# Cached keys turned by VectorE in 32x32 blocks in place of TensorE, in a decoder trunk on one core

## The chip, the cores and the metric

The kernel runs on one core of a Trainium2 chip. The core has five engines with instruction streams of their own: TensorE (PE; its weight loads are shown as PEld), VectorE (DVE), ScalarE (ACT), GpSimd (POOL) and SyncE (SP), which here only issues DMAs. They wait for each other by semaphores. The metric is the device time of one execution, in microseconds; lower is better.

## The reference

One inference step of two decoder layers with shared weights: a prompt of 1024 positions, and 8 samples with 8 new positions each. Layer 0 is a recurrent mixer and an FFN, layer 1 dilated windowed attention with 16 heads of 64 and an FFN. The change touches the attention of the samples. Each has 2048 cached keys and values:

```python
def dilated_gather(q, kall, vall, d, span):
    kidx = NP + jnp.arange(S)[:, None] - d * j[None, :]
    ...
    s = jnp.einsum('bshd,bsjhd->bhsj', q, kg) * (q.shape[-1] ** -0.5)
    s = s - alibi_slopes()[:, None, None] * (d * j)[None, None, :]
    ...
    o = jnp.einsum('bhsj,bsjhd->bshd', p, vg) / den.transpose(0, 2, 1)[..., None]
```

for three patterns (128 positions with stride 1, 512 with 4, 2048 with 16), combined by their softmax denominators. The kernel computes the union of the three as one softmax with a bias that holds slopes and multiplicities (`c_bs`), over 1280 cached positions and 8 new ones.

## The kernel before

All work is in one program with hand-written order. After the QKV projection (`s8_*`) comes the attention stage (`s9_*`). Its unit is a **slot** n: one pair of heads and one block of 128 queries of the prompt, qb = n % 8, so with (qb+1) x 128 key columns. There are 64 slots; slots -5 to -1 hold only sample work and the first queries and keys. Slots -5 to -2 are run by TensorE between the last 16 units of the projection (`run_in`, L2051). A slot has four phases on TensorE (`step`, L2529): the score matmuls of the block, then "turns" (128x128 transposes by matmul with the identity, up to four into one PSUM bank, `turn`, L2424), the product of the probabilities of slot n-2 with the values (`pv`), and sample work.

The **sample work** is laid over the slots: eight slots, s = 0 to 7, serve one sample b (`sample_slot`); s = (qb + 5) % 8. A sample has ten tiles of cached keys and ten of values, each 128 positions x 1024 numbers (all heads), 512 KB. In s = 0 to 4 four units of keys are turned (two tiles, eight transposes each, `turns`, L2277), ScalarE copies them to `smp_kt` (L2559), and TensorE scores them against a block matrix of the queries (`tile_scores`, L2472) in phase 3. VectorE adds the bias and takes minima (`piece`, L2651). In s = 5 the exponentials follow, in s = 6 the sample's probabilities are turned, in s = 7 they are multiplied with the ten value tiles (L2524), and `weigh` (L2657) normalizes in s = 0 of the next sample.

**The prompt's work by engine in slot n.** VectorE: `att_scores` reduction of both heads (L2677, with the bias and minimum), reciprocal, then copies of turned probabilities of slot n-1 (`take`, L2636), `piece`, and the output product of slot n-2 (L2708). ScalarE: copies of turned keys and queries in between the exponentials (L2583). GpSimd spreads reciprocals and issues loads of q, k, v and bias. The exponentials of n wait for the reduction of n, the turns of probabilities in slot n+1 for the exponentials of n.

**Turning banks.** Four PSUM banks serve the turns, but two of them hold scores while qb is 4 to 7, and are then given to turns from phase 3 on only. The plan gives each unit the bank that was longest unused:

```python
rest = () if n < 0 else (2,) if n >= NSLOT else (2, 3) if n % QT < 4 or f >= 3 else ()
x = min((0, 1) + rest, key=lambda b: last_use[b])
```

TensorE waits, before it turns into a bank, for the copy of what was there (`t_out`). Units are taken two per phase, in the order of the list that `turns` makes: the key units first, then those of the next pair's queries and keys, then the probabilities.

**The tiles' loads** are issued by SyncE in order of use (`cache_load`, L2363), into 10 buffers (12 near the end); a load waits for the last use of its buffer, and SyncE issues nothing behind it meanwhile. Key and value tiles 8 and 9 of a sample are put together from four loads each.

## Time and profile before

| | |
|---|---|
| time, median of 3 runs | 2775.1 us (2773.65 to 2776.35) |
| profiled execution | 2772.5 us, of which the trace's span is 2770.7 |
| TensorE busy | 2719.8 us |
| VectorE, ScalarE, GpSimd busy | 1737.5, 945.5, 97.6 us |
| DMA | 254.6 MB in 126388 packets |
| attention stage, slots from -1 on | from about 1500 us to about 1915 us |
| granted clock of TensorE, mean | 0.998 |

Busy times are shares of one profiled execution. A chain view follows the work back from the last instruction; a timeline lists merged runs of instructions with start and length; a windows view gives the busy time of each engine in a stretch, the granted clock, the mean busy share of the 16 DMA engines and GB/s.

### The profile page before, as it was taken

How to read it: one execution, taken by the hardware profiler on the slowest of the kernel's cores; microseconds unless marked ns; L12 is line 12 of the kernel's file. 1: busy time of each engine (PE TensorE's matmuls, PEld its weight loads, DVE VectorE, ACT ScalarE, POOL GpSimd, SP SyncE). 2: the span in 40 equal slices, each digit the busy share in tenths (PEclk: the TensorE clock that was granted, in tenths of full speed). 3: DMA queues.
4: the chain of work that ended last, by engine and by line, in shares of the span. 5: the costliest groups of instructions: out<-in, count | busy, mean ns of one | idle time of the engine just before them, and what ended most of it. 6: DMA issues, size and time to landing. Idle time of an engine off the chain costs nothing.

```text
span 2770.7 us, 56587 instructions
## 1 busy us (share of the span) xinstructions
PE 2719.8 (98%) x24537; PEld 2614.3 (94%) x24537; DVE 1737.5 (63%) x2858; ACT 945.5 (34%) x1690; POOL 97.6 (4%) x220
## 2 busy tenths in 40 slices
PE   7999999999999999999999999999999999999998
PEld 7998999999999999999998777777999999999998
DVE  5754536777777777755521666657377776766676
ACT  5543523322222222432223555554232222222222
POOL 1010000000000000000011111100000000000000
PEclk9999999999999999999999999999999999999999
DMA  5120120011111111133355776863101111111112
GB/s 201 34 82 13 64 99 31 31 50 58 46 47 46 47 47 47 62 127 95 95 176 193 258 268 218 281 238 127 61 16 47 47 47 46 47 47 47 57 52 80
DMA packets 126388, 254.64 MB, mean 92 GB/s; under 512 B 7617, under 2 KB 88725, under 8 KB 125632
## 3 DMA queue, kind: packets, MB, share of 16 engines
q1 hardware_dynamic: 112944, 189.26, 20.7%
q0 software_dynamic: 11888, 57.25, 5.9%
q10 hardware_dynamic: 1312, 4.52, 0.5%
q8 instruction: 196, 3.21, 0.5%
q14 instruction: 48, 0.39, 0.0%
HBM read 222.98 MB, written 28.02 MB: 91 GB/s over the span
## 4 chain that ended last, share of the span: by engine, by line
PE 92%; DVE 4%; ACT 2%; DMA 1%; issue 1%; POOL 0%; ACTq 0%; DVEq 0%; POOLq 0%
PE psum L1574 30%; PE psum L1629 18%; PE psum L483 14%; PE psum L224 11%; PE psum L1549 3%; PE psum L2459 2%; PE psum L2503 2%; PE psum L2419 2%; PE psum L2444 2%; PE psum L2472 1%; PE psum L2524 1%; DVE att_scores L2677 1%; DMA x_natural<-in_x_prompt 1%; PE psum L592 1%; PE psum L2448 1%
## 5 line engine op out<-in xcount | busy, mean ns | idle before, releaser
L1810 DVE TENSOR_TENSOR x_res<-x_res,psum 128x544 f32<-128x544 f32 x352 | 250.4, 719 | 155.4 <-PE psum L1629 155.4
L483 PE MATMUL psum<-w_hi,h_hi 128*128 128x256 f32 (+1 forms) x1152 | 327.1, 284 | 1.0 <-ACT qkv_tok L2074 1.0
L483 PE MATMUL psum<-w_hi,h_lo 128*128 128x256 f32 (+1 forms) x1152 | 323.6, 281 | 0.0
L483 PE MATMUL psum<-w_lo,h_hi 128*128 128x256 f32 (+1 forms) x1152 | 322.9, 280 | 0.0
L1629 PE MATMUL psum<-ffn_hi,ffn_unit_hi 128*128 128x272 f32 x1408 | 292.6, 289 | 1.8 <-DVE x_res L1810 1.4
L1629 PE MATMUL psum<-ffn_lo,ffn_unit_hi 128*128 128x272 f32 x1408 | 291.5, 288 | 0.0
L1629 PE MATMUL psum<-ffn_hi,ffn_unit_lo 128*128 128x272 f32 x1408 | 290.8, 288 | 0.0
L1574 PE MATMUL psum<-h_hi,ffn_unit_lo 128*128 128x272 f32 x1280 | 265.2, 288 | 0.0
L1574 PE MATMUL psum<-h_lo,ffn_unit_hi 128*128 128x272 f32 x1280 | 264.8, 288 | 0.0
L1574 PE MATMUL psum<-h_hi,ffn_unit_hi 128*128 128x272 f32 x1280 | 264.5, 288 | 0.0
L1629 PEld LDWEIGHTS psum<-ffn_hi,ffn_unit_hi 128*128 128x128 f32 x1408 | 220.7, 188 | 3.2 <-DVE x_res L1810 3.2
L1629 PEld LDWEIGHTS psum<-ffn_lo,ffn_unit_hi 128*128 128x128 f32 x1408 | 220.8, 188 | 0.0
L1629 PEld LDWEIGHTS psum<-ffn_hi,ffn_unit_lo 128*128 128x128 f32 x1408 | 220.7, 188 | 0.0
L483 PEld LDWEIGHTS psum<-w_hi,h_hi 128*128 128x128 f32 (+1 forms) x1152 | 215.1, 187 | 4.1 <-issue 1.8
L483 PEld LDWEIGHTS psum<-w_lo,h_hi 128*128 128x128 f32 (+1 forms) x1152 | 215.2, 187 | 0.0
L483 PEld LDWEIGHTS psum<-w_hi,h_lo 128*128 128x128 f32 (+1 forms) x1152 | 215.0, 187 | 0.0
L1574 PEld LDWEIGHTS psum<-h_hi,ffn_unit_hi 128*128 128x128 f32 x1280 | 201.0, 188 | 0.0
L1574 PEld LDWEIGHTS psum<-h_hi,ffn_unit_lo 128*128 128x128 f32 x1280 | 200.7, 188 | 0.0
L1574 PEld LDWEIGHTS psum<-h_lo,ffn_unit_hi 128*128 128x128 f32 x1280 | 200.6, 189 | 0.0
L1574 PE MATMUL psum<-ffn_t_hi,ffn_unit_lo 128*128 128x272 f32 x960 | 198.6, 288 | 0.0
L1574 PE MATMUL psum<-ffn_t_hi,ffn_unit_hi 128*128 128x272 f32 x960 | 198.6, 288 | 0.0
L1574 PE MATMUL psum<-ffn_t_lo,ffn_unit_hi 128*128 128x272 f32 x960 | 198.5, 288 | 0.0
(385 smaller groups left out, 5261.9 us busy)
## 6 DMA issues: line engine op xcount, KB each, us to landing
cache_tile<-in_cache_k SPq DMA_DIRECT2D x64, 512.0 KB, 8.2
cache_tile<-in_cache_v SPq DMA_DIRECT2D x64, 512.0 KB, 13.2
w_raw<-in_w_ffn_gate SPq DMA_DIRECT2D x22, 1024.0 KB, 5.1
w_raw<-in_w_ffn_up SPq DMA_DIRECT2D x22, 1024.0 KB, 5.1
w_raw<-in_w_ffn_down SPq DMA_DIRECT2D x22, 1024.0 KB, 4.8
w_raw<-in_w_in_att SPq DMA_DIRECT2D x12, 1024.0 KB, 7.1
w_raw<-in_w_in_rec SPq DMA_DIRECT2D x10, 1024.0 KB, 4.8
park_x<-x_res POOLq DMA_DIRECT2D x2, 4368.0 KB, 13.3
```

The source lines that it names most:

```text
L224: mm = pe.matmul(PS[:, bank + c, 0:n], st[slot][:, wc:wc + P], mv[:, k, c * CW:c * CW + n], start=(i < NCH), stop=(i >= 3 * NCH * nk - NCH))
L483: mm = pe.matmul(PS[0:n, bank, 0:BW], st[:, k, w:w + n], mv[slot][:, k * BW:(k + 1) * BW], start=(k == 0 and x == 0) if used is None else ...
L592: pe.matmul(PS[:, bank, 0:n], wt[:, j, :], XC[j % 2][:, c * CW:c * CW + n], start=True, stop=True).then_inc(g_in, 1)
L1549: mm = pe.matmul(PS[:, 2 * s + c, 0:CC], st[slot][:, k * BW + f * P:k * BW + (f + 1) * P], mv[:, k, t * TH + c * CC:t * TH + (c + 1) * CC] ...
L1574: mm = pe.matmul(PS[:, 2 * s + c, 0:CC], st[i % NU][:, k * P:(k + 1) * P], mv[:, k0 + k, t * TH + c * CC:t * TH + (c + 1) * CC], start=(fr ...
L1629: mm = pe.matmul(PS[:, 2 * s + c, 0:CC], st[(w0 + m // 2) % NU][:, x:x + P], mv[:, f, t * TH + c * CC:t * TH + (c + 1) * CC], start=(n < 2 ...
L1810: dve.tensor_tensor(x, x, pset(dset(g, i)), ALU.add).then_inc(s_res, 1)
L2419: mm = pe.matmul(PS[:, 2 * e + c // 512, 0:min(512, W - c)], q[p % 2][e * DH:(e + 1) * DH, qb * P:(qb + 1) * P], k[p % 2][e * DH:(e + 1) * ...
L2444: mm = pe.transpose(to[:, h * P:(h + 1) * P], TILE[BUF[j]][:, hp * P:(hp + 1) * P], ident[:, :])
L2448: mm = pe.transpose(to[:, t * P:(t + 1) * P], (QN, KN)[c // 2][:, 4 * (c % 2) + t, :], ident[:, :])
L2459: mm = pe.transpose(to[:, (k - c) * P:(k - c + 1) * P], SX[x % 2][:, e, y * P:(y + 1) * P], ident[:, :])
L2503: mm = pe.matmul(PS[c:c + NQ, 6, 0:P], VN[p % 2][:, x, c:c + NQ], PT[:, m % 2, c // DH * (qb + 1) + x, :], start=(x == 0), stop=(x == qb), ...
```

## The change

The key units vanish from TensorE's turns and from ScalarE's copies. VectorE turns each key tile with one instruction, 32x32 block by block, straight from the loaded tile into `smp_kt`. To make that fit, a key tile is loaded in another form: partition 32x+i holds head group x (four heads) of positions 32a+i, for four a. That takes four loads of 128 KB with pieces of 1 KB for every key tile. Rows and columns of the sample's queries, bias (`c_bs`), value product and output are reordered to match. VectorE turns two tiles at the end of its slots s = 7, 0, 1, 2, 3, for the next slot's scores; the first pair of sample 0 comes before slot -5. ScalarE takes the copies of the turned probabilities whose column offset is 4 or 12 blocks.

```diff
-        if b is not None:
-            units += [("k", i // 2, i % 2) for i in range(K_AT[s], K_AT[s + 1])]
...
-        return unit[0] not in ("p", "s") or unit[0] == "s" and unit[2] == 1
+        return unit[0] not in ("p", "s") or unit[0] == "s" and unit[2] == 1 or unit[0] == "p" and unit[2] % 8 == 4
...
+    def turned_at(b, x):
+
+        return 8 * b + x - 1 - LEAD
...
+            if u < 10:
+                for x in range(4):
+                    rows = sk[:, b, t, :, 256 * x:256 * x + 256] if t < 8 else sk[:, b, t:16:2, 3, 256 * x:256 * x + 256]
+                    sp.dma_start(TILE[BUF[j]][32 * x:32 * x + 32, :].rearrange("p (a d) -> p a d", a=4),
+                                 rows).then_inc(b_tile[BUF[j]], 16)
...
         def tile_scores(b, t):
-            bank, count = k_last(b, t)
-            pe.wait_ge(t_out[bank], count)
+            pe.wait_ge(b_kt, 10 * b + t + 1)
...
-            mm = sample_scores(lambda hp: SKT[:, t % 2, hp, :], (t % 2) * P, P)
+            mm = sample_scores(lambda x: SKT[:, t % 2, :, x, :], (t % 2) * P, P)
...
+        elif what == "p":
+            k = min(4, 2 * (x % QT + 1) - c)
+            act.activation(PT[:, x % 2, c:c + k, :].rearrange("p a w -> p (a w)"), bank[:, 0:k * P],
                            ACT.Copy).then_inc(t_out[TB_[g]], 1)
...
     def s9_dve(dve):
+        def keys(b, x):
+            if b or x:
+                dve.wait_ge(b_sc, 5 * b + x)
+            for t in (2 * x, 2 * x + 1):
+                j = 20 * b + t
+                dve.wait_ge(b_tile[BUF[j]], load_due(j))
+                dve.transpose(SKT[:, t % 2, :, :, :].rearrange("p a b w -> p (a b w)"), TILE[BUF[j]][:, :]).then_inc(b_kt, 1)
+
+        keys_at = {turned_at(b, x): (b, x) for b in range(DB) for x in range(5)}
+        dve.wait_ge(wl_done, B_QKV + N_QKV)
+        keys(0, 0)
...
                 dve.tensor_tensor(OX[:, m // QT, (m % QT) * P:(m % QT + 1) * P], PS[:, 6, 0:P], RS[:, n % 2, :],
                                   ALU.mult).then_inc(a_ox, 1)
+            if n in keys_at:
+                keys(*keys_at[n])
```

Beside this, the query and key rows of the samples are loaded by eight small DMAs of GpSimd in place of two, the four copies of `q_blocks` take 32 partitions each, and the two final copies of the samples' outputs become four each.

## Rows read from the trace of the kernel before

**Rows 1.** The page: busy time and count by engine; the chain by engine.
```profile
PE 2719.8 (98%) x24537; PEld 2614.3 (94%) x24537; DVE 1737.5 (63%) x2858; ACT 945.5 (34%) x1690; POOL 97.6 (4%) x220
...
PE 92%; DVE 4%; ACT 2%; DMA 1%; issue 1%; POOL 0%; ACTq 0%; DVEq 0%; POOLq 0%
```

**Rows 2.** Windows: one period, slot by slot; stretch, length, busy by engine, clock, DMA.
```profile
1661.04:1665.35 4.31, 4.31 (x82) 3.70 (x81) 3.13 (x11) 1.16 (x5) 0.30 (x1) 1.00 0.25 70
1665.35:1670.48 5.13, 5.13 (x93) 4.44 (x93) 4.00 (x13) 3.36 (x7) 1.30 (x6) 1.00 0.01 3
1670.48:1678.30 7.82, 7.82 (x117) 4.63 (x117) 4.24 (x14) 3.26 (x11) 0.29 (x1) 1.00 0.49 167
1678.30:1683.40 5.10, 5.10 (x97) 4.47 (x93) 3.32 (x9) 3.51 (x9) 0.29 (x1) 1.00 1.02 410
...
sum 51.49, PE 50.43 PEld 40.45 DVE 32.28 ACT 28.43 POOL 6.57; mean PE 6.30 PEld 5.06 DVE 4.03 ACT 3.55 POOL 0.82
```

**Rows 3.** The chain at the end of the projection: start, length, what.
```profile
1446.71 0.87 PE psum L2444 x8
...
1450.93 1.05 ACT smp_kt L2559 x2
...
1502.15 9.81 DMA out_v_sample<-qkv_tok
```

**Rows 4.** Timeline of slot s3: start, length, engine, line, what.
```profile
1698.04 1.09 PE L2444 MATMUL psum<-ident,cache_tile 128*128 128x128 f32 x8
1698.15 1.09 DVE L2677 CUSTOM_DVE_ANT_0 att_scores<-psum,att_bias 128x896 f32<-128x896 f32 x1 [0.81 <-PE psum L2419]
...
1701.01 1.29 DVE L2636 COPY att_pt<-psum 128x512 f32<-128x512 f32 x2 [0.67 <-PE psum L2459]
...
1701.24 0.27 PE L2496 MATMUL psum<-ident,att_rden_cols 128*128 128x128 f32 x1
...
1703.55 0.66 PE L2459 MATMUL psum<-ident,att_scores 128*128 128x128 f32 x4
```

**Rows 5.** Groups by line and form, 1380 to 2000 us: busy, mean ns, idle before.
```profile
L2444 PE MATMUL psum<-ident,cache_tile 128*128 128x128 f32 x640 | 87.6, 281 | 8.9 <-ACT smp_kt L2559 7.3 <-DMA cache_tile<-in_cache_k 1.5
L2559 ACT ACTIVATE smp_kt<-psum 128x512 f32<-128x512 f32 x160 | 86.9, 598 | 117.3 <-PE psum L2444 117.3
...
L2472 PE MATMUL psum<-smp_kt,smp_q_blocks 128*32 128x128 f32 x1280 | 43.1, 273 | 0.4 <-ACT smp_kt L2559 0.2
...
L2677 DVE CUSTOM_DVE_ANT_0 att_scores<-psum,att_bias 128x1024 f32<-128x1024 f32 x16 | 19.0, 1222 | 6.2 <-PE psum L2419 6.2
```

**Rows 6.** Groups by line and form, VectorE, whole span, from SBUF to SBUF.
```profile
L210 DVE TENSOR_TENSOR w_lo<-w_raw,w_hi 128x2048 fp32r<-128x2048 f32 x34 | 77.8, 2288 | 38.2 <-ACT w_hi L206 38.0
...
L1084 DVE TENSOR_TENSOR_SCAN lru_sa<-lru_a,lru_i 128x1092 f32<-128x1092 f32 x4 | 9.7, 2429 | 0.1
...
L1833 DVE TENSOR_SCALAR ffn_t<-x_res,vec_cols 128x544 f32<-128x544 f32 x8 | 3.6, 496 | 0.0
```

**Rows 7.** Timeline of slot s7, loads and VectorE's last; landing of all cached tiles.
```profile
1673.26 4.30 SPq L2385 DMA_DIRECT2D cache_tile<-in_cache_k  x8
...
1675.72 0.28 DVE L2708 TENSOR_TENSOR att_out<-psum,att_rden_rows 128x128 f32<-128x128 f32 x1
...
1677.60 1.86 SPq L2388 DMA_DIRECT2D cache_tile<-in_cache_k  x4
...
DMA to landing us min/median/max: 2.5/9.0/22.5
```

**Rows 8.** Windows around the store of v; the clock is the third number from the end.
```profile
1508.00:1512.00 4.00, 2.06 (x15) 1.05 (x13) 0.95 (x2) 0.60 (x3) 0.00 (x0) 1.00 1.04 339
1512.00:1516.00 4.00, 2.92 (x21) 2.27 (x25) 1.61 (x5) 2.28 (x5) 3.21 (x8) 0.60 1.01 269
```

**Rows 9.** The page, DMA issues: KB each and median us to landing.
```profile
cache_tile<-in_cache_k SPq DMA_DIRECT2D x64, 512.0 KB, 8.2
...
w_raw<-in_w_ffn_gate SPq DMA_DIRECT2D x22, 1024.0 KB, 5.1
```

More of the change, by code:

```diff
@@ L2133, in s8_pool @@
                     pool.wait_ge(v_dma[i], 32 * 4)
-                pool.dma_start(QSN[:, :], qtok[SEQ:SEQ + NS, :]).then_inc(b_ld, 16)
-                pool.dma_start(KSN[:, :], ks_).then_inc(b_ld, 16)
+                for x in range(4):
+                    w = slice(256 * x, 256 * (x + 1))
+                    for to, rows in ((QSN, qtok[SEQ:SEQ + NS, w]), (KSN, ks_[:, w])):
+                        pool.dma_start(to[:, :].rearrange("p (b a j) -> p b a j", b=HP, a=4)[:, :, x, :],
+                                       rows.rearrange("p (b j) -> p b j", b=HP)).then_inc(b_ld, 16)
                 pool.dma_start(QN[:, :, :], qp[:, :, 0:P]).then_inc(a_qk, 16)
@@ L2329, in last_turns @@
         return [(TB_[g], TC_[g]) for g in gs[-2:]]
-    def k_last(b, t):
-        s = max(i for i in range(8) if K_AT[i] <= 2 * t + 1)
-        return last_turn(8 * b + s - LEAD, "k", t)
+    def turned_at(b, x):
+        return 8 * b + x - 1 - LEAD
     def qk_last(p):
@@ L2341, in tile_used @@
         if u < 10:
-            s = max(i for i in range(8) if K_AT[i] <= 2 * u + 1)
-            n = 8 * b + s - LEAD
-            return n, max(i for i, x in enumerate(turns(n)) if x[0] == "k" and x[1] == u)
+            return turned_at(b, u // 2), 100 + u
         s, f = [x for x, steps in WEIGHED.items() if u - 9 in steps][0]
@@ L2359, in load_due @@
     def load_due(j):
-        return sum(64 if i % 10 >= 8 else 16 for i in range(j + 1) if BUF[i] == BUF[j])
+        return sum(64 if i % 20 < 10 or i % 10 >= 8 else 16 for i in range(j + 1) if BUF[i] == BUF[j])
     def cache_load(sp):
-        src = {x: a[x][0].rearrange("b (a r) h d -> a b r (h d)", r=16) for x in ("cache_k", "cache_v")}
+        sv = a["cache_v"][0].rearrange("b (a r) h d -> a b r (h d)", r=16)
+        sk = a["cache_k"][0].rearrange("b (a i r) h d -> i b r a (h d)", i=32, r=16)
         sp.wait_ge(v_park, 16)
@@ L2367, in cache_load @@
             b, u = divmod(j, 20)
[L2368 removed]
+            t = u % 10
             if j == 20 * DB - 2:
@@ L2379, in cache_load @@
                 if uo < 10:
-                    bank, count = k_last(bo, uo)
-                    sp.wait_ge(t_in[bank], count)
+                    sp.wait_ge(b_kt, 10 * bo + uo + 1)
                 else:
                     sp.wait_ge(b_vu, 10 * bo + uo - 9)
-            if t < 8:
-                sp.dma_start(TILE[BUF[j]][:, :], src[name][:, b, t, :]).then_inc(b_tile[BUF[j]], 16)
+            if u < 10:
+                for x in range(4):
+                    rows = sk[:, b, t, :, 256 * x:256 * x + 256] if t < 8 else sk[:, b, t:16:2, 3, 256 * x:256 * x + 256]
+                    sp.dma_start(TILE[BUF[j]][32 * x:32 * x + 32, :].rearrange("p (a d) -> p a d", a=4),
+                                 rows).then_inc(b_tile[BUF[j]], 16)
+            elif t < 8:
+                sp.dma_start(TILE[BUF[j]][:, :], sv[:, b, t, :]).then_inc(b_tile[BUF[j]], 16)
             else:
@@ L2399, in out1_lo, with by_group @@
         dve.tensor_tensor(AL[:, k, :], OX[:, k, :], AH[:, k, :].bitcast(F32), ALU.subtract).then_inc(a_lo, 1)
+    def by_group(rows, g):
+        return rows[:, :].rearrange("p (a g d) -> p a g d", a=4, g=4)[:, :, g, :]
     def att_pe(pe):
@@ L2438, in turn @@
                                       ident[0:NS, 0:NS])
-            elif what == "k":
-                j = 20 * sample_slot(n)[0] + x
-                pe.wait_ge(b_tile[BUF[j]], load_due(j))
-                for h in range(4):
-                    hp = 4 * c + h
-                    mm = pe.transpose(to[:, h * P:(h + 1) * P], TILE[BUF[j]][:, hp * P:(hp + 1) * P], ident[:, :])
             elif what == "qk":
@@ L2557, in take_act @@
                            ACT.Copy).then_inc(t_out[TB_[g]], 1)
-        elif what == "k":
-            act.activation(SKT[:, x % 2, 4 * c:4 * c + 4, :].rearrange("p a w -> p (a w)"), bank,
+        elif what == "p":
+            k = min(4, 2 * (x % QT + 1) - c)
+            act.activation(PT[:, x % 2, c:c + k, :].rearrange("p a w -> p (a w)"), bank[:, 0:k * P],
                            ACT.Copy).then_inc(t_out[TB_[g]], 1)
@@ L2572, in take_act @@
                 r = slice(e * DH, (e + 1) * DH)
-                dst = OX[r, :, S0 + 4 * x * DS:S0 + (4 * x + 4) * DS].rearrange("p k (b q) -> p b k q", q=DS)
-                src = bank[r, :].rearrange("p (b k e q) -> p b k e q", b=4, e=2, q=DS)[:, :, :, e, :]
-                op = act.activation(dst, src, ACT.Copy)
+                for y in range(2):
+                    dst = OX[r, :, S0 + 4 * x * DS:S0 + (4 * x + 4) * DS].rearrange("p (k y) (b q) -> p y b k q", y=2, q=DS)[:, y]
+                    src = bank[r, :].rearrange("p (b y e k q) -> p y e b k q", b=4, y=2, e=2, q=DS)[:, y, e]
+                    op = act.activation(dst, src, ACT.Copy)
             op.then_inc(t_out[TB_[g]], 1)
@@ L2730, in q_blocks @@
             done = 2 + 5 * b if b else 1
[L2731 to L2739 removed]
+            for x in range(4):
+                r = slice(32 * x, 32 * x + 32)
+                pool.wait_ge(b_qb, done)
+                done += 1
+                pool.tensor_copy(QB[r, :, x * DS:(x + 1) * DS], QTS[r, :, b * DS:(b + 1) * DS]).then_inc(b_qb, 1)
             pool.wait_ge(b_qb, done)
```

35 lines of the change are left out of this document (14 added, 21 removed).

## The prediction

> **What bounds the kernel now.** The page comes first: TensorE is busy for 98% of the span and makes up 92% of the chain that ended last, VectorE is busy for 63% [rows 1]. That is an average. The change touches only the attention stage, so the second view is one period of it, cut at TensorE's score matmuls. A period handles one sample in eight slots, which I call s0 to s7 as `sample_slot` does; s0 is the slot of query block 3. It lasts 51.49 us: TensorE is busy for 50.43, VectorE for 32.28, ScalarE for 28.43 [rows 2] (s5, s6, s7, s0, then the sum with s1 to s4). There are seven such periods (samples 1 to 7); the keys of sample 0 are turned earlier, among the QKV projection's matmuls [rows 3]. TensorE sets the pace, and at first sight work taken from it is gained. The third view, the timeline of s3, shows who hands what to whom: VectorE reduces the scores (1698.15), then copies turned probabilities (1701.01); TensorE turns, multiplies and scores around it [rows 4].
>
> **What TensorE loses.** 640 transposes of cached keys go [rows 5]. In s3 they hold TensorE from 1698.04 until the next turn near 1700.3, 2.3 us with a wait for ScalarE's copy in the middle [rows 4]. Read in the same way, s0 gives 1.7, s1 and s2 2.2 each, s4 2.5: 10.9 us a period, 76 us in seven, if nothing else bound. ScalarE loses 160 copies of 598 ns [rows 5].
>
> For sample 0 the chain shows eight groups of key turns of 0.87 us between projection matmuls, and one wait for ScalarE's two key copies (1.05 us, 1.5 with what surrounds them) [rows 3]. VectorE is nearly idle there, so its transposes are hidden: 7.0 + 1.5 = 8.5 us gained. In slot s4 of sample 0 the keys lie beside the store of v, whose landing takes 9.81 us and holds the chain [rows 3]: nothing gained. But the last value tiles of sample 0 can be loaded a slot earlier, out of this store's way. How much of the 9.81 that is no row tells; I take 2 us, from 0 to 4.
>
> **What VectorE gets and gives.** 80 transposes of 128x1024. No row shows one. Elementwise SBUF work of VectorE takes 2288 ns for 2048 elements, about one element per cycle; a scan, above it, takes 2429 ns for 1092, a one-source operation, below it, 496 ns for 544 [rows 6]. For 1024 elements that bounds a transpose by 0.7 and 2.3 us. I take 1.15 us in a row of instructions (the 1024-wide reduction is busy for 1222 ns [rows 5], of which 0.07 overlaps), 2.35 for a pair, since elementwise work is nearest in kind. The Trainium skill ("Vector Engine (DVE) Microarchitecture Reference", section 3.8, on the reshape front end) says that the 32x32 transpose sustains one element per cycle and lane; an estimate from it is 1.07 us plus overhead, and no row here shows it.
>
> `by_act` now gives ScalarE every second unit of turned probabilities (column offset 4 and 12): eight a period, six of 512 columns and two of 256, that took VectorE about 0.6 and 0.4 us in a row: 4.4. Per period VectorE then has 32.3 + 11.5 - 4.4 = 39.4 us, TensorE 51.5 - 10.9 = 40.6. Both would fit into 41. But the new work isn't spread: a pair stands at the end of s7, s0, s1, s2 and s3, in VectorE's strict order, ahead of the next slot's reduction. Behind it are queued that reduction, ScalarE's exponentials, and the copy of the first turned unit. And without key units the third unit of probabilities moves from phase 3 or 4 to phase 2, where only two turning banks exist (`rest` is empty for query blocks 4 to 7): it takes the bank of the first unit, which VectorE must free.
>
> **The walk through one period.** Zero is TensorE's start of s7. VectorE ends its slot at 5.5 (1675.72 and 0.28, less 1670.48) [rows 7]. The next sample's keys go into buffers that value matmuls free; the first key issue stands at 1673.26, or 2.8 [rows 7]. A key tile now is four issues of 0.43 to 0.47 us, as four-part tiles are [rows 7], so tile 0 is issued by 4.6 and tile 1 by 6.3; with the shortest landing, 2.5 [rows 7], the second transpose ends at 9.5. TensorE's s0 begins at 7.8; its scores are there at 8.8, so 0.7 us is lost.
> - s0: reduction, weighing, one copy, and behind TensorE's key scores (until 12.6) piece and output, then a pair: 15.7.
> - s1: reduction 1.65, copy 0.6, piece and output 0.65, pair 2.4: 21.0. TensorE waits a few tenths.
> - s2: TensorE has scored and turned two units by 19.8. Now the third unit: VectorE's reduction 1.9, copy 0.6, TensorE's third unit 0.3, then spreading, product and key scores 2.2, VectorE's piece and output 0.65, pair 2.35: 29.0.
> - s3: the same with 2.2, 0.65, 0.55, 2.3 (1701.24 to 1703.55 [rows 4]), 0.7 and 2.4: 37.8.
> - s4: reduction 2.45, copy 0.65, third and fourth unit 0.75, product and key scores 2.5: TensorE starts s5 at 44.2. No pair stands here.
> - s5: 4.3 as before [rows 2]. s6: 5.1 before; ScalarE now copies the fourth unit before its exponentials and so comes 1 us later to the next queries, which holds two of four banks: 5.8. End: 54.3.
>
> That is 54.3 against 51.5: s0 and s1 give back 1.9 us, s2, s3 and s4 take 1.7, 1.3 and 1.1 more than now, s6 0.7. The key turns that go had filled the time in which scores are reduced, exponentiated and copied. Seven periods: 7 x 2.8 = +19.5.
>
> **Smaller parts.** The first pair of period 1 comes under full DMA load, +1. The two final copies become four each, +1. The strided moving operands I take at nothing, since the column counts stay; 5% on the 1280 score matmuls, which run four at a time at 273 ns [rows 5], would be some 2 us. GpSimd's eight loads of query and key rows in place of two cost it 6 us of issue, two projection blocks ahead of their use: 0.
>
> **TensorE's clock.** In s2, s3 and s4 the walk leaves TensorE idle for 3.7, 3.3 and 3.6 us. The trace has one comparable place: in 1508 to 1512 it is busy for 2.06 of 4 us, and the 4 us from 1512 on are granted 0.60 [rows 8], that is 3.2 us at 1.2 GHz in place of 2.4, 1.6 us of work lost if all of it lies on the path. 21 gaps make 34 us at most; I count a quarter, 8. The Trainium skill ("TensorE: Matmul & The Clock Gate", Part 1) says that the array idles at 1.2 GHz and that activity releases it; by that rule taking filler work away can cost speed, which is a rival below.
>
> **Sum.** Profiled execution before: 2772.5. -8.5 (sample 0) - 2 (store) + 19.5 (periods) + 1 + 1 + 8 (clock) = +19, so 2791.5. The median before is 2775.1, 2.6 above the profiled one: 2794.
>
> **The rivals.**
> - *VectorE has the room.* A transpose near 0.7 us: 10 x 0.45 a period, and shorter gaps, so no clock loss: 7 x 4.5 + 8 = 40 less, 2754. With VectorE off the path altogether: 76 gained, none lost: 2794 - 76 - 19.5 - 8 = 2690. For: the one-source row of 496 ns [rows 6], 12 us of room in the sums. Against: the order of the walk. Faster; 0.23.
> - *Hand-overs shorter than walked.* 1.5 us a period and no clock loss: 18 less, 2776. For: each wait was taken at its longest. 0.20, of it 0.11 within the bound of no change, 0.09 below it.
> - *The clock falls in each gap*: + 26, 2820. For: [rows 8]. Against: the short gaps of now keep 1.00 [rows 2]. 0.07.
> - *Keys come late.* Pieces of 1 KB, four issues. With 8.2 us of landing, the median of key tiles now [rows 9], in place of 2.5, each period loses up to 5.7: + 40, 2834. For: the DMA share is 1.02 in s0 [rows 2]. Against: in s7 it is 0.49, and 1 MB of weights, in 1 KB rows too, lands in 5.1 [rows 9]. 0.05.
> - *Slow transposes*, 2.3 us: 70 x 1.15 = 80 more, 2874. 0.05.
>
> **How the numbers follow.** The forecast has 0.40, with its own range 2781 to 2808, all of it slower. Within 0.2% is 2769.5 to 2780.7, about what a measurement of this kernel can tell from no change. Faster: 0.23 + 0.09 = 0.32. Same: 0.11. Slower: 0.40 + 0.07 + 0.05 + 0.05 = 0.57. The range, 2750 to 2834, leaves out the slow transposes and the far part of the first rival.
>
> **What would show it.** A VectorE group of 80 transposes near 1.2 us each; in s2, s3 and s4 TensorE's third turn of probabilities released by VectorE's copy after some 3 us of idle; waits for key tiles in s7 alone, 1 to 2 us each; the projection's end 8 us earlier; granted clocks under 1.00 in the stage, or not. A period near 50 would give the first rival, one near 41 its far end and prove the walk wrong; above 57 the last three.

## The result, and the profile after

The changed kernel takes 2828.3 us (median of 4 runs, 2824.15 to 2828.59), the kernel before 2775.7 (4 runs, 2773.65 to 2777.47): 1.0187 times as long, with an interval of 1.0174 to 1.0199. The forecast was 2794. The sign was right and the time lies in the range, but the change was forecast at +19 us and measured at +52.6. The profiled execution took 2828.6 us, its span is 2826.8. One execution of a later kernel, the split pair, took 5667 us with TensorE busy for 5619.5 of them, and no time given for that kernel uses it.

From the page of the kernel after: TensorE's, VectorE's and ScalarE's busy time, and the chain by engine. Beside them, the transposes from the view by line and form (busy us, mean ns, idle before).

```profile
PE 2685.1 (95%) x23897; PEld 2578.6 (91%) x23897; DVE 1792.3 (63%) x2874; ACT 896.1 (32%) x1598; POOL 102.4 (4%) x226
...
PE 85%; DVE 8%; ACT 2%; DMA 2%; issue 1%; SPq 1%; POOL 0%; ACTq 0%; DVEq 0%; POOLq 0%
```
```profile
L2631 DVE STREAM_TRANSPOSE smp_kt<-cache_tile 128x1024 f32<-128x1024 f32 x80 | 95.4, 1223 | 29.3 <-DMA cache_tile<-in_cache_k 29.3
```

Two differences read off these lines and [rows 1] account for the whole. TensorE is idle for 2826.8 - 2685.1 = 141.7 us, against 2770.7 - 2719.8 = 50.9 before: 90.8 more. It is busy for 34.7 less. The sum, +56.1, is the growth of the span. But the key turns that went were 87.6 us of its busy time [rows 5], so the work that stayed took 87.6 - 34.7 = 52.9 us longer than before, with the same instructions. That is the clock: over 1512 to 1950 us the windows grant 0.88 in the mean, and 1.00 in the kernel before.

The view of waits of TensorE, 1500 to 1980 us (us in total, times, longest), names the idle time, and the one of VectorE a third thing.

```profile
PE psum L2462 <- DVE att_pt L2653: 70.1, 23, 3.8
PE psum L2477 <- DVE smp_out L2674: 25.7, 7, 6.5
```
```profile
DVE smp_kt L2631 <- DMA cache_tile<-in_cache_k: 29.3, 14, 6.0
```

There are 23 waits for VectorE's copy of a first turned unit: three a period in s2, s3 and s4, of 2.5 to 3.8 us, 68 us together, and two short ones of 2 us together; seven for `weigh` in s0, of 2.6 to 6.5 us; and 14 in which VectorE itself waits for a key tile, two a period.

Windows of the kernel after, slots s7, s0, s1, s2 and s3 of the third period (stretch, length, busy by engine, clock, DMA share, GB/s), to be held against [rows 2], whose clocks are 1.00 in every slot shown:

```profile
1630.96:1638.78 7.82, 7.82 (x117) 4.63 (x116) 5.16 (x15) 3.25 (x11) 0.29 (x1) 1.00 0.45 117
1638.78:1645.77 6.99, 4.39 (x81) 3.55 (x77) 4.44 (x10) 2.06 (x6) 0.29 (x1) 0.87 0.94 234
1645.77:1650.48 4.71, 4.71 (x82) 3.98 (x77) 4.59 (x13) 1.43 (x4) 0.00 (x0) 0.83 1.13 231
1650.48:1660.16 9.68, 5.91 (x91) 4.85 (x88) 6.27 (x13) 3.88 (x10) 2.96 (x5) 0.87 1.09 255
1660.16:1668.90 8.74, 5.90 (x103) 4.86 (x101) 6.32 (x13) 3.04 (x6) 1.13 (x2) 0.95 1.05 362
```

TensorE starts the slots of this period at 0 (s7), 7.8, 14.8, 19.5, 29.2, 37.8, 48.6, 52.9, and the next at 58.7. With the slots of the kernel before and the walk's differences from them, the walk had about 0, 7.8, 12.4, 17.3, 26.0, 34.7, 44.2, 48.5, 54.3. So 2.4 of the 4.4 us between the walk and the trace are lost in s0, where the second key tile is turned at 11.1 rather than 9.5 and TensorE then works at a lower clock; the rest lies in s2 and s4, 1.0 and 1.3 longer than walked.

This is the shortest of the periods. From one period's first key load to the next's they last 61.4 us in the mean, and 52.3 in the kernel before: 9.1 more, where the walk had 2.8. Seven times 9.1, less the 7.6 us that the projection's tail gives, is the 56 us by which the span grew.

The timeline of the kernel after shows what happens in s0: the loads, the two transposes with their waits, the wait for `weigh` and the 32 key scores behind it, which take 1.84 us (1.06 where the first experiment's trace shows them at a clock of 1.00).

```profile
1633.73 19.16 SPq L2387 DMA_DIRECT2D cache_tile<-in_cache_k  x36
...
1637.86 1.25 DVE L2631 STREAM_TRANSPOSE smp_kt<-cache_tile 128x1024 f32<-128x1024 f32 x1 [1.38 <-DMA cache_tile<-in_cache_k]
1640.78 1.25 DVE L2631 STREAM_TRANSPOSE smp_kt<-cache_tile 128x1024 f32<-128x1024 f32 x1 [1.67 <-DMA cache_tile<-in_cache_k]
...
1643.83 1.84 PE L2477 MATMUL psum<-smp_kt,smp_q_blocks 128*32 128x128 f32 x32 [2.60 <-DVE smp_out L2674]
```

A further timeline, of s2, shows the typical wait: TensorE's third unit stands 3.77 us behind a copy that VectorE reaches only after the pair and the reduction.

```profile
1655.87 0.67 DVE L2653 COPY att_pt<-psum 128x512 f32<-128x512 f32 x1
...
1656.60 0.44 PE L2462 MATMUL psum<-ident,att_scores 128*128 128x128 f32 x2 [3.77 <-DVE att_pt L2653]
...
1660.83 2.36 DVE L2631 STREAM_TRANSPOSE smp_kt<-cache_tile 128x1024 f32<-128x1024 f32 x2
```

### The profile page after: what moved, and what is told of

It is laid out like the page before. It is cut to its first block, busy times and chain, and to the rows that moved or that the text cites. A ratio compares the mean times of both kernels' runs of the same rounds, so it can differ in the third digit from the quotient of the medians.

```text
span 2826.8 us, 55309 instructions
## 1 busy us (share of the span) xinstructions
PE 2685.1 (95%) x23897; PEld 2578.6 (91%) x23897; DVE 1792.3 (63%) x2874; ACT 896.1 (32%) x1598; POOL 102.4 (4%) x226
## 4 chain that ended last, share of the span: by engine, by line
PE 85%; DVE 8%; ACT 2%; DMA 2%; issue 1%; SPq 1%; POOL 0%; ACTq 0%; DVEq 0%; POOLq 0%
PE psum L1575 29%; PE psum L1630 17%; PE psum L484 14%; PE psum L225 11%; PE psum L1550 3%; PE psum L2507 2%; DVE att_scores L2694 2%; DVE smp_kt L2631 2%; PE psum L2462 2%; PE psum L2477 2%; DMA cache_tile<-in_cache_k 1%; PE psum L2428 1%; ACT att_scores L2589 1%; PE psum L2528 1%; SPq L2387 1%
## 6 DMA issues: line engine op xcount, KB each, us to landing
cache_tile<-in_cache_v SPq DMA_DIRECT2D x64, 512.0 KB, 13.6
```

## The experiments

All are edits of the kernel after unless the text says otherwise. The excerpts show the lines that matter; semaphore counts, the plan of buffers and other lines that follow from them are left out. The kernel before, run beside them, had medians from 2774.7 to 2775.5 us.

**ScalarE takes the first and third unit.** The wait is for a unit that VectorE copies; here it is ScalarE's, which takes 32 copies more than in the kernel after.

```
-  unit[0] == "p" and unit[2] % 8 == 4
+  unit[0] == "p" and unit[2] % 8 == 0
```

> Changed kernel, with ScalarE taking the turned probability units at column offset 0 and 8 instead of 4 and 12. The third unit then waits for a ScalarE copy that stands before the exponentials, not for VectorE's copy behind a pair of transposes and a reduction. Theory A (the order of the hand-over is the cause, as walked in the prediction: the 23 waits of TensorE for VectorE's copies, 70 us): in s2 and s3 these waits vanish, in s4 only the fourth unit still waits; the period falls from 61 to 50 to 53 us, time 2765 to 2785, and the granted clock in the stage rises since the gaps go. Theory B (the amount of VectorE work is the cause, whatever the order): VectorE is as busy, the waits move to TensorE's key scores or to the next slot's scores; time within 15 us of 2828. Theory C (late key tiles are the cause): the same as B, with the 29 us of waits for key tiles unchanged or larger.

Measured 2791.5 us (ratio to before 1.0058, 1.0043 to 1.0073). The waits for VectorE's copies fell from 70.1 us (23 times) to 25.9 (7, one a period). The period, from first key load to first key load, fell from 61.4 us on average to 55.4. The kernel before has 52.3, measured in this way. So 37 us of the loss hung on this edit. It also takes 20 us of copies off VectorE (busy for 1772.6 us, 1792.3 after), which this run alone doesn't separate from the order; the split pair below does. The time lies 6 us above what was expected: the clock stayed low, 0.984 in the mean.

**One load for a key tile.** The four loads of 32 partitions become one of 512 KB.

```
+  if t < 8:
+      sp.dma_start(TILE[BUF[j]][:, :], sk1[:, b, t, :]).then_inc(b_tile[BUF[j]], 16)
```

> Changed kernel, with key tiles 0 to 7 of each sample loaded as before the change: one load of 512 KB in rows of 4 KB. The keys then stand in the wrong order in the tile, so that the samples' attention is computed on permuted keys; all instructions are the same. VectorE waited 29 us for key tiles in the changed kernel, 4.2 us a period where the walk had 1.9, and the loads' issues take 19 us of SyncE's time a period. Theory A (late keys are the second term that was sized too small): the waits fall from 29 to under 12 us, the time by 15 to 30 us, to about 2805; TensorE's waits for VectorE's copies, 70 us, stay. Theory B (the four small loads are as good; the waits come from VectorE asking a slot earlier): waits stay near 29, time within 6 us of 2828. Theory C (the form of loads is the main cause of the whole loss): time falls under 2790.

Measured 2813.9 us (1.0139, 1.0124 to 1.0154): 14.4 less than after, just short of theory A. VectorE's waits for keys fell from 29.3 us to 16.7, not under 12, TensorE's for `weigh` from 25.7 to 13.0, and the period to 58.9. Of the 13.6 us by which the span shrank, 7.0 are TensorE's idle time and 6.6 its busy time: with shorter gaps there is less slow clock too.

**Idle transposes in the gaps.** TensorE transposes the identity into an unused part of a bank ahead of the third unit in s2, s3 and s4 (20 times) and ahead of the value product and the key scores in s0 (14 times).

```
+  if what == "p" and i == 2 and 0 <= n < 56 and n % QT in (5, 6, 7):
+      filler(pe, n, 20)
...
+  if s == 0 and b and f == 3:
+      filler(pe, n, 14)
```

> Changed kernel, with idle work for TensorE: 20 transposes of the identity (about 2.3 us) before its wait for the third unit of probabilities in s2, s3 and s4, and 14 (1.6 us) in s0 before the value product, into columns of a PSUM bank that nobody reads. The work computed stays the same. Theory A (the clock falls in the gaps; it is the third term sized too small, some 3 us a period): the granted clock of the stage returns from 0.85 to 0.95 to 1.00 nearly everywhere, and although TensorE has 60 us more to do, the time falls by 10 to 25 us, to 2803 to 2818. Theory B (the clock is low only while TensorE waits anyway): the clock rises and the time stays within 6 us, or rises by up to 10 where the filler outlasts a gap.

Measured 2795.5 us (1.007, 1.0054 to 1.0087) at a mean clock of 0.996: 33 us gained by adding 518 matmuls, 7.5 more than theory A allowed. The page and the view by line of this kernel, then the line of key scores of the kernel after:

```profile
PE 2703.0 (97%) x24415; PEld 2603.2 (93%) x24415; DVE 1792.3 (64%) x2874; ACT 895.9 (32%) x1598; POOL 102.5 (4%) x226
```
```profile
L2414 PE MATMUL psum<-ident 128*128 128x128 f32 x518 | 61.1, 273 | 0.0
...
L2485 PE MATMUL psum<-smp_kt,smp_q_blocks 128*32 128x128 f32 x1120 | 38.9, 281 | 11.9 <-DVE smp_out L2684 11.9
```
```profile
L2477 PE MATMUL psum<-smp_kt,smp_q_blocks 128*32 128x128 f32 x1120 | 50.0, 335 | 25.7 <-DVE smp_out L2674 25.7
```

TensorE's own work now takes 2703.0 - 61.1 = 2641.9 us, 43.2 less than in the kernel after and 9.7 more than in the kernel before (2719.8 - 87.6 = 2632.2). Its idle time together with the filler is 91.5 + 61.1 = 152.6, 10.9 more than after. That is the account of the clock: 43 us of slow work go, and 11 of them come back as waiting, because VectorE was late anyhow. The key scores show it on one line: 335 ns, then 281, where [rows 5] have 273.

**ScalarE's share taken away.** `by_act` as in the kernel before.

```
-  or unit[0] == "p" and unit[2] % 8 == 4
```

> Changed kernel without the share of ScalarE in the copies of turned probabilities: VectorE takes them all, as before the change. It gets 4.4 us more a period. Theory A (order): in s2 and s3 only what stands on the loop counts; the second unit's copy comes behind the first and delays the third unit's copy and, in s4, the fourth unit: 1.5 to 3 us a period, time 2838 to 2850. Theory B (amount of VectorE work): all 4.4 us count, 31 us, time about 2860. If the time doesn't rise, ScalarE's share was worth nothing.

Measured 2823.5 us (1.0174, 1.0154 to 1.0195), 4.9 less than after; the two executions, 2820.7 and 2826.2, reach into the range of the kernel after, so that no gain is shown, but no loss either. It was expected to be slower by 10 us and more. ScalarE's share of the copies is worth nothing in the form that it has: TensorE's 23 waits are there in either kernel (72.5 us here, 70.1 after), for they are for the first unit, which is VectorE's in both.

**First and third unit, and idle transposes.** The waits that are left in the first experiment are filled in s4 and s0: the edit of the first, and

```
+  if what == "p" and i == 3 and 0 <= n < 56 and n % QT == 7:
+      filler(pe, n, 20)
...
+  if s == 0 and b and f == 3:
+      filler(pe, n, 14)
```

> The kernel after with two things at once: ScalarE copies the first and third unit of turned probabilities instead of the second and fourth, and TensorE does idle transposes of the identity (extra work, no use to the result) ahead of the fourth unit of the one slot where it still waited 3.3 us, and in the first slot ahead of the keys' scores. Alone, the first of these gave 2791.5 us at a mean clock of 0.984, the idle transposes alone 2795.5 at 0.996. Theory A: the longer way of the period and the slow clock are two losses, and what is left of the clock in the first (0.984 against 0.998) is worth some 10 to 20 us: 2772 to 2782. Theory B: with the shorter gaps the clock costs nothing more, and idle transposes only add work: 2789 to 2796.

Measured 2788.3 us (1.0044, 1.0029 to 1.0059), clock 0.993: nearer to theory B. Only 3 us are gained over the first experiment; this run has VectorE waiting 44.5 us for key tiles, against 27.2 there, so part of what was filled may have become late keys; no run shows that apart.

**One load, and idle transposes.** The edits of the second and the third experiment together.

> The kernel after with the key tiles 0 to 7 in one load of 512 KB each (the keys then stand in another order in the scores, so the computation is changed) and the idle transposes in the gaps of TensorE. Alone they gave -14.4 and -33 us. Theory A: late keys and slow clock are separate losses: 2828 - 14 - 33 = 2781, at most 2785. Theory B: the late keys only cost because TensorE then ran slowly, so that the two overlap: 2792 to 2797. What is left over 2775.3 is then the order of VectorE's work alone.

Measured 2783.0 us (1.0029, 1.0017 to 1.0041): theory A. The two losses nearly add: 14.4 and 33 alone, 45.3 together. Without them the kernel is 7.5 us above the one before, with the gain in the projection's tail already taken off, and the period lasts 54.8 us against 52.3. That is about what VectorE's order of work costs. TensorE still waits here behind the filler, 21 times in s2, s3 and s4 for 1.1 to 1.7 us, and the granted clock over 1512 to 1950 is 1.00.

**The pair split.** VectorE turns the second tile of a pair behind the next slot's reduction and first copies. The instructions are the same.

```
+  if f == 1 and n - 1 in keys_at:
+      keys(*keys_at[n - 1], (1,))
...
-  keys(*keys_at[n])
+  keys(*keys_at[n], (0,))
```

> The kernel after, with the second transpose of each pair moved from the end of the slot to behind the first copies of turned probabilities of the next slot; the same instructions, the same number of waits, another order on VectorE. Theory A (what costs is that reduction and first copies stand behind two transposes in a row, 2.3 us, and not the amount of VectorE's work): the slots of the first half of a period fall back to within 0.5 us each of their length before, 2778 to 2800. Theory B (VectorE simply has too much to do in these slots, in whatever order): 2818 to 2835.

Measured 2789.9 us (1.0045, 1.0028 to 1.0061). The trace that is read here is of one more execution of the same kernel:

> The same kernel as the split pair (second transpose of a pair behind the next slot's first copies), for its trace. Theory A (order): the 23 waits of TensorE for the copy of a first unit, 70 us in the kernel after, are all but gone (under 20 us), the granted clock of the whole is 0.99 or more, and what is left over the kernel before (14 us) is the loads: holes in TensorE's own stream and key tiles that come late. Theory B: the waits are still there, only shorter (over 40 us).

Measured 2786.7 us, mean clock 0.990. TensorE's waits in this kernel:

```profile
PE psum L2462 <- DVE att_pt L2653: 46.6, 23, 2.2
PE psum L2477 <- DVE smp_kt L2631: 19.2, 14, 1.8
```

VectorE does the same work, and 38 us are gone, so it isn't the amount of VectorE's work that costs but where it stands (theory B of the first text falls). But the waits are only shortened, by 1.0 us each in the mean where one transpose takes 1.2 (theory B of the second text is nearer), and 14 new ones for the second tile appear. Shorter gaps also mean less slow clock: TensorE is busy for 2668.0 us, 17 less than after.

**Split, and one load.** The split pair with the edit of the second experiment.

> The split pair together with the one load of 512 KB for each of the key tiles 0 to 7 (keys in another order, so the computation is changed). The split alone measured 2789.9, and the loads of 1 KB pieces alone put 15.8 us on the kernel before. Theory A (order and loads are separate and are all there is): 2772 to 2778, the time of the kernel before, less what the projection's tail gives. Theory B (VectorE's transposes still cost through something else): 2783 to 2790.

Measured 2784.9 us (1.0033, 1.0020 to 1.0046): 2 to 5 us gained, not 14. Theory B. With the pair split the second tile is wanted later, so that a late landing is probably mostly hidden; VectorE's waits for keys are 14.4 us here and 15.9 with four loads.

**Split, and ScalarE on the first and third unit.** The split pair with the edit of the first experiment.

> The split pair, with ScalarE copying the first and third unit of turned probabilities instead of the second and fourth; same result as the kernel after, so it is also a candidate. Theory A (with the pair split, no copy is late any more): nothing gained, 2785 to 2792. Theory B (the second transpose now delays the reduction or a first unit by another 1 to 2 us in some slots): 2775 to 2784.

Measured 2773.8 us (0.9994, 0.9984 to 1.0004): level with the kernel before, and 1.2 us under the lower edge of theory B. Each of the two edits alone gave 37 to 38 us, together 54.5. The profiled execution was a quick one, 2765.6 us, with a period of 51.9 where the kernel before has 52.3. The waits for copies are down to 9.3 us; what is left is the second tile:

```profile
PE psum L2477 <- DVE smp_kt L2631: 28.8, 27, 1.8
PE psum L2462 <- DVE att_pt L2653: 9.3, 7, 1.3
```

**Products between the two key tiles.** In the kernel of the last experiment TensorE scores the even tile, does the product of probabilities and values, then scores the odd tile.

```
+  for t in SCORED.get((s, f), ())[0:1]:
+      tile_scores(b, t)
   if 2 <= n and f == PV_AT.get(s, 1):
       pv(n - 2)
-  for t in SCORED.get((s, f), ()):
+  for t in SCORED.get((s, f), ())[1:2]:
       tile_scores(b, t)
```

> The split pair with ScalarE on the first and third unit (2773.8 us), in which TensorE now does the products of turned probabilities and values between the scores of the even and of the odd key tile, not ahead of both. In the trace of that kernel TensorE waited 27 times for the odd tile's transpose, 28.8 us in all and 1.8 at most, and the products last 0.9 to 1.5 us. Theory A: the products fill these waits, and nothing else becomes late: 2748 to 2760, faster than the kernel before. Theory B: the later products delay the outputs, and with them ScalarE and VectorE, by as much: 2768 to 2778.

Measured 2773.7 us (0.9992, 0.9983 to 1.0): theory B. The waits for the odd tile fell to 17.6 us, but those for `weigh` rose from 5.5 to 10.7, and TensorE's idle time is the same, 101.8 us and 100.2.

**The loads alone, on the kernel before.** TensorE turns the keys as before; only the loads are the change's.

```
+  if u < 10:
+      for x in range(4):
+          rows = sk[:, b, t, :, 256 * x:256 * x + 256] if t < 8 else ...
+          sp.dma_start(TILE[BUF[j]][32 * x:32 * x + 32, :].rearrange("p (a d) -> p a d", a=4), rows)...
```

> The kernel before, in which only the loads of the key tiles are those of the change: each as four loads of 32 partitions in pieces of 1 KB, issued one after the other by SyncE (the turned tiles are then other rows, so the computation is changed), and still turned by TensorE. Theory A: the loads are hidden behind TensorE here too, and cost nothing by themselves: 2773 to 2780. Theory B: four issues and four times the packets delay the keys whoever turns them, and TensorE then waits for them: 2788 to 2800.

Measured 2791.4 us (1.0059, 1.0044 to 1.0074): +16, theory B, though the keys hardly come late (TensorE waits 4.0 us for them, against 1.5). Instead there are holes in TensorE's own stream, in the midst of a group and with no releaser: 8, of 11.4 us together, against 3 of 2.6 us in the kernel before. In the span (16.8 us longer) TensorE is idle for 12.5 us more and busy for 4.3 more. Two of the holes, from its timeline:

```profile
1604.61 0.38 PE L2465 MATMUL psum<-ident,att_scores 128*128 128x128 f32 x2 [2.31 <-issue]
...
1615.10 0.44 PE L2465 MATMUL psum<-ident,att_scores 128*128 128x128 f32 x2 [1.94 <-issue]
```

**Four loads with pieces of 4 KB, on the kernel before.** This separates packets from issues.

```
+  if u < 8:
+      for x in range(4):
+          sp.dma_start(TILE[BUF[j]][32 * x:32 * x + 32, :],
+                       src[name][32 * x:32 * x + 32, b, t, :]).then_inc(b_tile[BUF[j]], 16)
```

> The kernel before, in which each of the key tiles 0 to 7 is loaded by four loads of 32 partitions in pieces of 4 KB, so with the change's number of issues and the packets of the kernel before; same result as the kernel before. With pieces of 1 KB the same kernel measured 2791.4 us, and its TensorE had 8 holes in its own stream of instructions, 11.4 us, against 3 and 2.6 us before. Theory A (what costs is the packets, the transfers that share the chip's queues with everything else): 2774 to 2779. Theory B (SyncE's issuing, four instructions of some 0.5 us a tile): 2786 to 2793.

Measured 2789.3 us (1.0053, 1.0040 to 1.0066): theory B. The size of the pieces is not what costs: four loads with pieces of 4 KB cost nearly what four with pieces of 1 KB do, 14 and 16 us. Loads of 32 partitions cost, four for one. The holes are at the same instructions as in the last experiment:

```profile
1606.84 0.38 PE L2463 MATMUL psum<-ident,att_scores 128*128 128x128 f32 x2 [2.59 <-issue]
...
1618.79 0.44 PE L2463 MATMUL psum<-ident,att_scores 128*128 128x128 f32 x2 [2.17 <-issue]
```

The queue of these loads, from the page (packets, MB, share of the time of 16 engines) of this kernel, then of the kernel before:

```profile
q1 hardware_dynamic: 116016, 189.27, 22.2%
```
```profile
q1 hardware_dynamic: 112944, 189.26, 20.7%
```

The same bytes hold the DMA engines longer, for 22.2% of 2787.3 us in place of 20.7% of 2770.7: 45 us on all sixteen. Over 1512 to 1950 us their mean share is 0.80 in this kernel, 0.83 with pieces of 1 KB and 0.68 in the kernel before, at nearly the same GB/s (228 and 232). Theory B named SyncE's issuing. No run separates it from this longer hold on the DMA engines: both come with four loads for one.

**Idle transposes in s0 only.** Of the third experiment's two edits, the second.

> The kernel after with the idle transposes of the identity only in the first slot of each period, ahead of the keys' scores, and not in the three slots with the waits for a first unit. With both places filled it measured 2795.5 us (28 to 33 us faster than the kernel after). Theory A: each gap costs its own slow stretch after it; one of four or five gaps of a period is in this slot: a fifth to a third of the gain, 2817 to 2822. Theory B: the wait of the first slot is what starts the slow clock of the whole half period (0.83 to 0.87 in the two slots behind it): 2795 to 2805. Theory C: the later gaps bring it on by themselves: 2825 to 2829.

Measured 2822.6 us (1.0169, 1.0156 to 1.0183; single executions from 2817.8 to 2825.6), 5.7 less than after. Theory B falls. The time lies 0.6 us above theory A and 2.4 below theory C, and its spread doesn't part those two; that TensorE's own work is 12.2 us shorter than in the kernel after (2685.7 busy, less 12.8 of filler) speaks for A. By difference the three gaps in s2 to s4 carry the other 27 of the 33 us.

The trace of the kernel after can be counted gap by gap. Of its 28 gaps in s0, s2, s3 and s4, of 2.5 to 6.5 us, 23 bring a stretch with a granted clock of 0.50, which begins in the gap or within 1.1 us of its end; the other five are all gaps of s3, of 2.5 to 2.9 us. The work that took 52.9 us longer is 1.9 us for each of the 28.

**The best of it.** Split, first and third unit, products between, and idle transposes at the two places of a period behind which the clock still fell in some periods (13 in s0, 11 in s4). On top of the edits named:

```
+  if what == "p" and i == 3 and 0 <= n < 56 and n % QT == 7:
+      filler(pe, n, 11)
...
+  if s == 0 and b and f == 3:
+      filler(pe, n, 9)
   for t in SCORED.get((s, f), ())[0:1]:
       tile_scores(b, t)
+  if s == 0 and b and f == 3:
+      filler(pe, n, 4)
```

> The kernel with the split pair, ScalarE on the first and third unit and the products between the two key tiles (2773.7 us, mean clock 0.992), with idle transposes of the identity in the two places of a period behind which its clock still fell to 0.5: nine ahead of the first key tile's scores and four behind them in the first slot, eleven ahead of the fourth unit in the slot with all sixteen transposes. Same result as the kernel after. Theory A: the slow stretches of 4 to 6 us behind these two waits are a loss of their own, 7 periods by one to two stretches that lose 1 to 2 us each: 2755 to 2766, faster than the kernel before. Theory B: VectorE sets the length of these slots, and TensorE's slow stretches only fill time in which it would wait: 2770 to 2778.

Measured 2766.6 us (0.9974, 0.9963 to 0.9984): faster than both kernels (by 0.26% against the one before), and 0.6 us above the upper edge of theory A. The windows of the kernel without these transposes (around s4's wait), then of the one with them:

```profile
1650.00:1652.00 2.00, 0.91 (x15) 0.75 (x18) 1.15 (x5) 2.00 (x4) 0.29 (x1) 0.90 1.02 334
1652.00:1654.00 2.00, 2.00 (x36) 1.31 (x30) 1.44 (x2) 0.65 (x2) 0.00 (x0) 0.50 1.00 373
1654.00:1656.00 2.00, 2.00 (x52) 1.72 (x46) 0.12 (x1) 0.28 (x1) 0.00 (x0) 0.75 1.04 410
```
```profile
1644.00:1648.00 4.00, 3.76 (x62) 3.04 (x66) 3.50 (x8) 2.92 (x6) 0.29 (x1) 1.00 1.03 357
1648.00:1652.00 4.00, 4.00 (x107) 3.56 (x99) 1.82 (x9) 0.87 (x2) 0.30 (x1) 1.00 1.02 404
```

A wait of 1.34 us is followed by two microseconds at 0.50, that is 1.2 of 2.4 GHz, and two that are at 0.75 in the mean; with the wait filled, there is no such stretch. But this wait isn't typical of its length. In the same trace, 17 us earlier, TensorE waits for 1.49 us and the clock stays (stretch, length, PE busy, clock, DMA share, GB/s):

```profile
1632.00:1634.00 2.00, 0.88 (x18) 1.00 1.17 221
1634.00:1636.00 2.00, 2.00 (x20) 1.00 0.96 294
```

Four other waits of s4, of 1.31 to 1.36 us, keep 1.00 too. What tells the one from the others no run shows. Over the whole span TensorE's own work is 15.8 us shorter than without these transposes (2679.0 less 22.2 of filler, against 2672.6), and idle time and filler together are 5.7 longer than its idle time was.

**The same with one load.** With the edit of the second experiment added.

> The same kernel with one load of 512 KB for each of the key tiles 0 to 7 (keys in another order, so the computation is changed). Alone on the kernel before, the loads by four cost 14 to 16 us; in the kernel after a single load gave 14.4 back; with the pair split, only 2 to 5. Theory A: the cost of the loads is holes in TensorE's own stream and transfers that come late, and it is back once TensorE is busy throughout: 10 to 16 us below the kernel of this call with loads by four. Theory B: with the pair split the tiles are wanted later, and the loads cost nothing any more: within 4 us of it.

Measured 2757.9 us (0.9942, 0.9928 to 0.9955): 8.7 below the last, between the theories. It tells what the loads cost; with its keys in another order it isn't a kernel to use. The three prices of the four loads rise as TensorE idles less: 2 to 5 us where it is idle for 117 us, 9 where for 84, 14 to 16 on the kernel before, where for 51. That the one brings the other is an inference from three points. In the kernel after, the 14 were another thing, late keys: its view of waits shows no hole without a releaser.

## Why the prediction was right in sign and short in size

- *The walk.* Right where it put the loss. The place was right (third unit, released by VectorE's copy, in s2, s3 and s4), and so was the size: walked 3.7, 3.3 and 3.6 us, measured 3.8, 2.8 and 3.4 in the third period, and 74 us walked in seven against 68. With the gaps filled and the keys in one load, the period was 2.5 us longer than before, where the walk had 2.8. The total of idle time agrees in part by luck: 13.7 us more a period, 96 in seven, were walked, 90.8 measured in the whole span, but in s0 the walk had a wait of 0.7 us and the trace has 25.7 us of them in seven periods. The forecast's own sign for the last three rivals, a period above 57, came: 61.4. It was two of the three, the clock and the keys. The rival that gives VectorE the room has fallen, though its busy time is 38.9 us in a period of 58.7: the split pair gained 38 us without taking any work away.
- *The transposes.* 1.15 us in a row were taken, 2.35 for a pair, between bounds of 0.7 and 2.3 us [rows 6]; measured 1223 ns each, 2.36 for a pair. The trace agrees with the reference on VectorE's microarchitecture in the Trainium skill, which has one element per cycle and lane ("Vector Engine (DVE) Microarchitecture Reference", section 3.8): the estimate of 1.07 us that the prediction drew from it is most of the 1223 ns.
- *ScalarE's share.* The walk took 4.4 us of copies a period off VectorE and let it count. Taken back, the kernel was no slower (4.9 us less in two executions). What counts is the first unit.
- *The clock.* This is the term that failed. 21 gaps by 1.6 us, [rows 8], made 34 at most, and a quarter was taken, 8, for which the prediction names no row. Filled gaps gave back 33, of which 6 belong to the gaps of s0, which the sum had not counted, and 27 to its 21. The row was nearly right (1.9 us a gap) and the quarter was wrong: 23 of 28 gaps are followed by a slow stretch, and most of that lies on the path. What was not seen either is that the slow stretches last through the short slot behind them (0.83 in s1, which has no wait at all). In busy time it is 52.9 us; 43.2 of it go with the filler and 10.9 come back as waits. The rival "the clock falls in each gap" (+26, given 0.07) was this one. The Trainium skill's rule that the array idles at 1.2 GHz and is released by activity ("TensorE: Matmul & The Clock Gate", Part 1) had been weighed as a rival; the trace agrees with it in the windows shown. Its length alone doesn't tell whether a gap brings the clock down: 23 of 28 of 2.5 to 6.5 us did in the kernel after, one of five of s4 of 1.3 to 1.4 us in the kernel with the products between, and none of 21 of 1.1 to 1.7 us in the one with one load and idle transposes.
- *The keys' loads.* Second term that failed. Beyond the walk they were counted at 1 us for the whole. The tiles came late twice a period, 29.3 us of waits by VectorE, and one load for a tile gave back 14.4. What was sized wrong is the landing, which the walk took at 2.5 us, the shortest on record. The eight issues of a first pair go as walked: in the third period the last of them begins 6.0 us after TensorE's start of s7, and 0.43 us is the median of an issue. (Over all 36 of the period it is 0.53, as now and then one takes 1.5.) But the last load of the second tile lands 3.0 to 7.0 us after its issue in the seven periods, 3.8 in the median. A single load for the second tile is complete 5.2 to 7.2 us after the pair's first issue, four loads 7.0 to 11.6: issuing four for one costs time as well, and the walk had that part. So the rival "keys come late" named the right thing, a landing of more than 2.5 us, with too large a price, 40 us. The experiment with pieces of 4 KB says nothing against it: it was made on the kernel before, whose loss is another. Measured with those two terms out, the kernel is 7.5 us above the one before; the forecast without its clock term and its late first pair was 19 - 8 - 1 = 10. So these two make the miss: 45.3 us together against 9, 36 over their terms, less 2.5 by which the rest was too high, is the 33.6 that was missed.
- *The tail of the projection.* 8.5 us were forecast for the keys of sample 0. The landing of `out_v_sample` holds the chain from 1494.52 in the kernel after, from 1502.15 before: 7.6. That it would be shorter by 2 us did not happen:

```profile
1494.52 9.77 DMA out_v_sample<-qkv_tok
```

- *Final copies, GpSimd's loads, strided operands.* No run tells them apart. The strided operand costs nothing that shows: in the run with one load and idle transposes the key scores take 273 ns, as in the kernel before [rows 5].

## What to carry to other kernels

When work is taken off the busiest engine, walk what stood between the hand-overs before counting the gain: its instructions were filling a wait, and a copy queued behind the moved work now ends it. A gap of some three microseconds that opens on TensorE is to be priced at its length and, in full, at the slow stretch behind it (1.9 us a gap here); gaps of 1.7 us and less mostly cost their length alone here. If a long gap can't be closed, idle matmuls in it pay. Ask of every engine which of its pieces the other one waits for next, and give that one to the engine that is free.

## What was not expected of the hardware

On the kernel before, loading a [128, 1024] tile by four loads of 32 partitions costs more than one load, with either size of pieces: 14 us over 64 tiles for pieces of 4 KB, 16 for 1 KB (where tiles 8 and 9 have them too).

The holes in TensorE's stream recur at fixed distances. In both kernels with four loads the two holes shown are 123 matmuls apart, and the first lies at the third transpose of the same group, where the kernel before has one of 1.49 us. These windows are of the kernel with the loads alone, from the first hole to the second and from there to a third, of 0.32 us:

```profile
1604.55:1615.05 10.50, 8.24 (x123) 1.00 1.03 386
1615.05:1622.80 7.75, 7.41 (x123) 1.00 0.73 171
```

123 matmuls with their weight loads are 246 instructions. The Trainium skill says that an engine's instructions come in blocks of 256 by a DMA queue of its own, and that this is mostly hidden ("Runtime: NRT & Kernel Launch", section "Instruction fetch mechanics"). The distance fits with a few waits counted in; hidden it is not here: the hole behind a stretch with a DMA share of 1.03 is 1.94 us long, the one behind 0.73 is 0.32.

The traces show the blocks themselves. The page has a queue for them, with the same 196 packets, of 16 KB each, in the kernel before and in both with four loads:

```profile
q8 instruction: 196, 3.21, 0.5%
```

Between 1500 and 1960 us every hole without a releaser that is longer than 0.3 us, six or seven in the kernels with four loads and three in the kernel before, ends 1.2 to 1.7 us after the end of one of these packets. At the two holes shown first, packets ran from 1602.15 to 1603.31 and from 1612.75 to 1613.84; TensorE went on at 1604.61 and 1615.10. So the holes are waits for a block of instructions. That the blocks are late because the DMA engines are full is an inference: no run changed the instructions' place or took the other transfers away.
